# Transposes of q, k, softmax weights and the second half's x moved from TensorE to DMA in a hybrid attention and convolution layer on eight cores

## The reference, cut to what matters

```
h = RMSNorm(x) * pre_norm_g
p = h @ w_in + b_in          # q 1024 | k 128 | v 128 | attn gate 1024 | glu value 1024 | glu gate 1024 | conv gate 1024
attn = softmax over a causal window of 128 keys, with a sink logit per head,
       of rope(q) rope(k)^T / 8, times v; 16 query heads of 64, 2 key/value heads; times silu(attn gate)
hc   = value * sigmoid(gate); causal depthwise convolution of 31 taps + b_dw; LayerNorm over channels;
       silu; @ w_pw + b_pw; times silu(conv gate)
y = concat([attn, hc]) @ w_out + b_out
out = x + RMSNorm(y) * post_norm_g
```

## Time and profile before

| | us |
|---|---|
| median of 3 runs | 1105.13 (1103.37 to 1117.91) |
| profiled execution, its own time | 1108.99 |
| its span, core 2, first to last instruction | 1107.5 |
| span of the other cores | 1089.4 to 1099.1 |

### The profile page before, as it was taken

How to read it: one execution, slowest core, us unless ns; L and a number is a source line. 1 busy time by engine, 2 the same in 40 slices (tenths; PEclk the granted TensorE clock), 3 DMA queues, 4 the chain that set the end, 5 groups by cost and what they waited for, 6 DMA issues and landing times.

```text
span 1107.5 us, 17820 instructions; the slowest of 8 cores (1089.4 to 1107.5 us)
## 1 busy us (share of the span) xinstructions
PE 1034.8 (93%) x6848; PEld 543.7 (49%) x6906; DVE 531.1 (48%) x921; ACT 412.2 (37%) x1013; POOL 212.8 (19%) x215
## 2 busy tenths in 40 slices
PE   3799999899999999999999999989999999999996
PEld 1556444555555444445544644455655544444443
DVE  3566301466665355446636650045776636533434
ACT  2452112556555445034511212155565544402111
POOL 0260000134543320000000000012455341000000
PEclk9899999999999999999999999999999999999999
DMA  8874334655566589979499303344645657992445
GB/s 184 277 113 79 57 48 76 127 116 117 128 136 131 147 191 159 192 200 204 91 171 185 78 10 67 76 102 108 177 122 140 152 141 174 165 180 41 81 76 109
DMA packets 26533, 141.92 MB, mean 128 GB/s; under 512 B 5985, under 2 KB 6369, under 8 KB 15969
## 3 DMA queue, kind: packets, MB, share of 16 engines
q0 software_dynamic: 8784, 80.74, 43.1%
q1 hardware_dynamic: 17666, 60.04, 17.7%
HBM read 171.72 MB, written 32.51 MB: 184 GB/s over the span
## 4 chain that ended last, share of the span: by engine, by line
PE 73%; DMA 7%; SPq 6%; DVE 6%; ACT 3%; issue 3%; POOL 1%; ACTq 0%; DVEq 0%; POOLq 0%
PE psum L1144 19%; PE psum L775 10%; PE psum L1023 10%; SPq L152 6%; DMA arena<-arena 5%; PE psum L635 5%; PE psum L1113 5%; PE psum L869 4%; PE psum L818 4%; PE psum L828 4%; PE psum L631 3%; PE psum L593 2%; ACT arena L928 2%; PE psum L530 1%; PE psum L1182 1%
## 5 line engine op out<-in xcount | busy, mean ns | idle before, releaser
L1144 PE MATMUL psum<-arena 128*128 128x512 bf16 x939 | 207.2, 379 | 1.1
L1144 PEld LDWEIGHTS psum<-arena 128*128 128x128 bf16 x960 | 93.6, 98 | 111.3
L818 PE MATMUL psum<-arena 128*128 128x352 bf16 (+1 forms) x768 | 124.3, 316 | 0.0
L828 PE MATMUL psum<-arena 128*128 128x352 bf16 (+1 forms) x768 | 120.9, 311 | 3.4 <-ACT arena L831 3.3
L928 ACT ACTIVATE arena<-psum,arena 128x128 f32<-128x128 f32 x256 | 93.9, 367 | 61.4 <-DVE arena L918 43.6
L1023 PE MATMUL psum<-arena 128*128 128x512 bf16 x500 | 110.9, 379 | 4.3 <-ACT arena L1027 3.0
L775 PE MATMUL psum<-arena 128*128 128x512 bf16 x502 | 113.6, 387 | 0.5
L828 PEld LDWEIGHTS psum<-arena 128*128 128x128 bf16 x768 | 74.8, 98 | 42.9 <-issue 5.3
L818 PEld LDWEIGHTS psum<-arena 128*128 128x128 bf16 x768 | 72.5, 99 | 47.6 <-issue 12.7
L907 DVE COPY_PREDICATED psum<-arena,psum 128x1024 f32<-128x1024 uint16 x32 | 38.7, 1208 | 117.7 <-PE psum L901 117.7
L942 POOL TENSOR_TENSOR arena<-arena 128x1024 bf16<-128x1024 f32 x32 | 60.5, 1892 | 140.7 <-DVE arena L941 140.7
(11 more groups left out here) (129 smaller groups left out, 1282.9 us busy)
## 6 DMA issues: line engine op xcount, KB each, us to landing
arena<-w_in POOLq DMA_DIRECT2D x12, 2048.0 KB, 16.0
arena<-x_ext SPq DMA_DIRECT2D x18, 1024.0 KB, 10.6
arena<-w_in POOLq DMA_DIRECT2D x16, 1024.0 KB, 10.4
out<-arena POOLq DMA_DIRECT2D x15, 1024.0 KB, 9.2
arena<-w_out POOLq DMA_DIRECT2D x6, 2048.0 KB, 20.2
arena<-arena SPq DMA_DIRECT2D x64, 66.0 KB, 2.0
arena<-arena SPq DMA_DIRECT2D x64, 65.9 KB, 2.0
arena<-arena SPq DMA_DIRECT2D x64, 65.9 KB, 2.3
```

The lines of the kernel that those rows point to most:

```text
L818: cx.op('pe', lambda e, k=k: e.matmul(out=bank[bv][:, 0:n], lhsT=wbuf.ap[:, k, o:o + 128], rhs=xv[:, k, st:st + n], start=(k == 0), stop=( ...
L828: cx.op('pe', lambda e, k=k: e.matmul(out=bank[bg][:, 0:n], lhsT=wbuf.ap[:, k, o + 128:o + 256], rhs=xv[:, k, st:st + n], start=(k == 0), ...
L1144: cx.op('pe', lambda e, k=k: e.matmul(out=bank[b], lhsT=MIX.ap[:, k, j * 128:(j + 1) * 128], rhs=wo[n][k][0].ap[:, wo[n][k][1], :], start= ...
```

## The change

- `p1_b` for the second half: one DMA on SP from `xn` (128 x 2048) to XT1, `transpose=True`, in place of 16 transposes, an ACT copy and a DVE copy.
- `kv_b` and `q_b`, both halves: one transposing DMA on SP (128 x 256, 128 x 512) in place of 2 or 4 transposes and an ACT copy.
- Softmax weights: a new step `att_d` issues a transposing DMA of 128 x 1024 on SP from `pn` to a new tile `ptc` (two of them; the arena grows by 2 KB). `att_t` then has no PE part: its two DVE operations read `ptc` from SBUF, write `ptb` and, in place, `ptc`. For even units `att_d` comes right after `att_n`. For odd units it comes after the tick that follows the taps, and after 12 of the 16 shuffle DMAs; the other 4 follow it.
- PSUM bank 3 joins banks 0 and 1 in the rotation of GLU groups and taps.
- New DMA semaphores: 2 for q, 3 for k, 2 for the softmax weights, one for x.

The first half's x keeps its TensorE transposes. The whole diff:

```
--- before.py
+++ after.py
@@ -279,7 +279,7 @@
         O_KV = O_Z + 16384
         O_CV = O_KV + 7168
         O_AT = O_CV + 17920
-        ARENA = O_AT + 24576
+        ARENA = O_AT + 26624
         arena = cx.sb("arena", [128, ARENA], U8)
         BT = [T(f"blk{i}") for i in range(ARENA // BLK)]
 
@@ -370,6 +370,10 @@
         s_wo = [cx.dsem("wo0"), cx.dsem("wo1")]
         s_o = [cx.dsem("o%d" % i) for i in range(3)]
         s_x4 = cx.dsem("xr4")
+        s_qt = [cx.dsem("qt%d" % i) for i in range(2)]
+        s_kt = [cx.dsem("kt%d" % i) for i in range(3)]
+        s_pt = [cx.dsem("pt%d" % i) for i in range(2)]
+        s_xt = cx.dsem("xtr")
         s_rs = cx.dsem("rs")
         s_wh = [[cx.dsem("wh%d%d" % (i, h)) for h in range(2)] for i in range(2)]
         s_cp = cx.dsem("cp")
@@ -524,6 +528,11 @@
             return p1_n(s, j, n, bufs)
 
         def p1_b(s, j, xn):
+            if s == 1:
+                c0 = xcol(s, j)
+                cx.dma('sp', XT1.ap[:, :, c0:c0 + 128], xn.ap, s_xt, R=[xn],
+                       W=[xt_t[1][j]] + (xt_t[0] if j == 1 else []), transpose=True)
+                return
             bA, bB = nbank(), nbank()
             for k in range(16):
                 bb = bA if k < 8 else bB
@@ -600,17 +609,12 @@
                 cx.op('dve', lambda e: e.tensor_copy(
                     out=V.ap[:, j, :, :], in_=kf.ap[:, 128:256].rearrange("p (h d) -> p h d", d=64)),
                     R=[kf], W=[V_t[j]])
-                return kb
-
-            def kv_b(j, kb):
-                bt = nbank()
-                for g in range(2):
-                    cx.op('pe', lambda e, g=g: e.transpose(
-                        out=bank_bf[bt][:, g * 128:(g + 1) * 128], in_=kb.ap[:, g, :, :].rearrange("p a d -> p (a d)"),
-                        identity=ident_bf), R=[kb, cst_bf], W=[BK[bt]])
-                cx.op('act', lambda e: e.copy(
-                    out=kT.ap[:, :, j * 128:(j + 1) * 128],
-                    in_=bank_bf[bt][:, 0:256].rearrange("p (g n) -> p g n", n=128)), R=[BK[bt]], W=[kT_t[j]])
+                return kb, n
+
+            def kv_b(j, kbn):
+                kb, n = kbn
+                cx.dma('sp', kT.ap[:, :, j * 128:(j + 1) * 128], kb.ap.rearrange("p g a d -> p (g a d)"), s_kt[n % 3],
+                       R=[kb], W=[kT_t[j]], transpose=True)
 
             def q_h(b, j, wp, h):
                 c0 = xcol(s, j)
@@ -640,18 +644,12 @@
                     R=[BK[b], bq], W=[f])
                 rope(f.ap.rearrange("p (h d) -> p h d", d=64), b_.ap.rearrange("p (h d) -> p h d", d=64),
                      8, s * 8 + j, r1, r2, [f], [b_], E, 'pool' if E == 'pool' else 'dve')
-                return b_
-
-            def q_b(g, j, b_):
-                bt = nbank()
-                for t in range(4):
-                    cx.op('pe', lambda e, t=t: e.transpose(
-                        out=bank_bf[bt][:, t * 128:(t + 1) * 128], in_=b_.ap[:, t * 128:(t + 1) * 128],
-                        identity=ident_bf), R=[b_, cst_bf], W=[BK[bt]])
-                cx.op('act', lambda e: e.copy(
-                    out=MIX.ap[:, 4 * g:4 * g + 4, (j - 1) * 128:j * 128],
-                    in_=bank_bf[bt][:, 0:512].rearrange("p (t n) -> p t n", n=128)),
-                    R=[BK[bt]], W=[mix_t[4 * g + t][j - 1] for t in range(4)])
+                return b_, n
+
+            def q_b(g, j, bn):
+                b_, n = bn
+                cx.dma('sp', MIX.ap[:, 4 * g:4 * g + 4, (j - 1) * 128:j * 128], b_.ap, s_qt[n % 2],
+                       R=[b_], W=[mix_t[4 * g + t][j - 1] for t in range(4)], transpose=True)
 
             lag = []
 
@@ -785,7 +783,8 @@
 
             eb = [mk(O_AT + i * 4096, [8, 128], F32) for i in range(2)]
             pn = [mk(O_AT + 8192 + i * 2048, [8, 128], BF16) for i in range(2)]
-            ptb = [mk(O_AT + 12288 + i * 2048, [8, 128], BF16) for i in range(2)]
+            ptb = mk(O_AT + 12288, [8, 128], BF16)
+            ptc = [mk(O_AT + o_, [8, 128], BF16) for o_ in (14336, 24576)]
             ub = [mk(O_AT + 16384 + i * 2048, [512], F32) for i in range(2)]
             vb = [mk(O_AT + 20480 + i * 2048, [512], F32) for i in range(2)]
             ysum = [mk(O_MIX + 24576 + i * 2048, [512], F32) for i in range(2)]
@@ -793,7 +792,7 @@
             sq = [mk(O_MIX + 20480 + i * 2048, [512], F32) for i in range(2)]
             mixhi = [t for k in range(8, 16) for t in mix_t[k]]
 
-            rot["list"] = [0, 1]
+            rot["list"] = [0, 1, 3]
             if s == 0:
                 GRP = [(96, 0, 352), (448, 352, 352), (800, 704, 352)]
             else:
@@ -853,12 +852,12 @@
                     in1=cp[:, C_WDW + c * 32:C_WDW + (c + 1) * 32].rearrange("p (m g) -> p m g", g=4).unsqueeze(3)
                     .broadcast_to([128, 8, 4, 32]), op=ALU.mult), R=[cpb_], W=[dg])
 
-            def conv_shuffle(c):
+            def conv_shuffle(c, part):
                 hg = hglu[c % 2]
-                for g in range(4):
-                    for i in range(4):
-                        cx.dma('sp', rs.ap[32 * i:32 * (i + 1), g, 0:HW - i], hg.ap[32 * g:32 * (g + 1), i:HW],
-                               s_rs, R=[hg], W=[rs], group=True)
+                for q in (range(12) if part == 0 else range(12, 16)):
+                    g, i = q // 4, q % 4
+                    cx.dma('sp', rs.ap[32 * i:32 * (i + 1), g, 0:HW - i], hg.ap[32 * g:32 * (g + 1), i:HW],
+                           s_rs, R=[hg], W=[rs], group=True)
 
             def conv_taps(c, t2):
                 dg = diag[c % 2]
@@ -888,7 +887,7 @@
                     cx.op('pool', lambda e: e.tensor_tensor(out=qss.ap, in0=qss.ap, in1=sb_.ap, op=ALU.add),
                           R=[sb_, qss], W=[qss])
 
-            OB, TB = 2, 3
+            OB = 2
             SBK = [BK[i] for i in range(4, 8)]
             SV = psum[:, 2048:4096].rearrange("p (h k i) -> p h k i", h=8, k=2)
 
@@ -943,20 +942,20 @@
                     out=pu.ap, in0=eu.ap, in1=st["rden"].ap.unsqueeze(2).broadcast_to([128, 8, 128]), op=ALU.mult),
                     R=[eu, st["rden"]], W=[pu])
 
+            def att_d(ui):
+                pu, pc = pn[ui % 2], ptc[ui % 2]
+                cx.dma('sp', pc.ap, pu.ap.rearrange("p h k -> p (h k)"), s_pt[ui % 2], R=[pu], W=[pc], transpose=True)
+
             def att_t(ui):
-                pu = pn[ui % 2]
-                for h in range(8):
-                    cx.op('pe', lambda e, h=h: e.transpose(
-                        out=bank_bf[TB][:, h * 128:(h + 1) * 128], in_=pu.ap[:, h, :], identity=ident_bf),
-                        R=[pu, idn], W=[BK[TB]])
-                for i, m in ((0, mprev_bf), (1, mcur_bf)):
-                    cx.op('dve', lambda e, i=i, m=m: e.tensor_tensor(
-                        out=ptb[i].ap, in0=bank_bf[TB].rearrange("p (h q) -> p h q", q=128),
-                        in1=m.unsqueeze(1).broadcast_to([128, 8, 128]), op=ALU.mult),
-                        R=[BK[TB], cst_bf], W=[ptb[i]])
+                pc = ptc[ui % 2]
+                for o_, m in ((ptb, mprev_bf), (pc, mcur_bf)):
+                    cx.op('dve', lambda e, o_=o_, m=m: e.tensor_tensor(
+                        out=o_.ap, in0=pc.ap, in1=m.unsqueeze(1).broadcast_to([128, 8, 128]), op=ALU.mult),
+                        R=[pc, cst_bf], W=[o_])
 
             def att_o(ui):
                 g, j = units[ui]
+                pp = (ptb, ptc[ui % 2])
                 for kb in range(2):
                     kt = j - 1 + kb
                     for eh in range(2):
@@ -964,9 +963,9 @@
                             q4 = eh * 2 + dq
                             cx.op('pe', lambda e, kb=kb, kt=kt, eh=eh, dq=dq, q4=q4: e.matmul(
                                 out=bank[OB][32 * q4:32 * q4 + 32, :], lhsT=V.ap[:, kt, g, 32 * dq:32 * dq + 32],
-                                rhs=ptb[kb].ap[:, 4 * eh:4 * eh + 4, :].rearrange("p h q -> p (h q)"),
+                                rhs=pp[kb].ap[:, 4 * eh:4 * eh + 4, :].rearrange("p h q -> p (h q)"),
                                 start=(kb == 0), stop=(kb == 1), tile_position=(0, 32 * q4)),
-                                R=[V_t[kt], ptb[kb]], W=[BK[OB]])
+                                R=[V_t[kt], pp[kb]], W=[BK[OB]])
                 cx.op('dve', lambda e: e.tensor_tensor(
                     out=MIX.ap[:, 4 * g:4 * g + 4, (j - 1) * 128:j * 128],
                     in0=bank[OB].rearrange("p (t q) -> p t q", q=128), in1=arena_gate(g, j), op=ALU.mult),
@@ -986,6 +985,8 @@
                 for lag_, f in ((5, att_o), (4, att_t), (2, att_n), (0, att_s)):
                     if (n - lag_) >= 0 and (n - lag_) % 2 == 0 and (n - lag_) // 2 < 16:
                         f((n - lag_) // 2)
+                        if f == att_n and n % 4 == 2:
+                            att_d((n - lag_) // 2)
 
             wgc = [None, None]
             tick()
@@ -1008,12 +1009,14 @@
                 if c > 0:
                     conv_taps(c - 1, 0)
```

(6 more changed lines are left out.)

## The result

The changed kernel takes **1196.2 us** (median of 4 runs, 1194.4 to 1199.1), against 1104.25 of the kernel before beside it: ratio 1.083, 95% interval 1.078 to 1.088. The forecast was 1115 us in a range of 1078 to 1152: the change costs nine times what was forecast, and the time lies 44 us outside the range. Executions in which the cores of a die ran at a lower granted clock than the others are left out of all times here.

A forecast was written before the change was run, and what follows sets the result against it. The prediction took PE, busy 1034.8 of 1107.5 us, as the bound. Its terms, -9.0 - 7.4 - 2.3 - 4.5 + 13.8 + 19.5 = +10.1 us, on 1105.1 gave 1115 us, range 1078 to 1152.

The forecast's parts named there:

- x, -9.0 us: Second half's x in the output stage: eight sets of transposes leave PE and nothing there waits for XT, -9.0 us.
- The model of a DMA beside a load: GLU stage: a DMA issued behind the weight load takes 6.9 or 10.4 us, plus 0.9 for its bytes.
- q -7.4 and k -2.3: Projections: q saves 0.23 us in each of 32 tiles, -7.4; k saves half of 4.6 us, -2.3.
- rival 3: First half's k and q stages: late DMAs hold k and q buffers until PE waits, +10, 1125 us; chance 0.08.
- Second half's odd units, +13.8: Second half's GLU blocks: DMA behind the weight load lengthens the period from 21.8 to 24.1 us, six blocks, +13.8.
- First half's odd units, +19.5: First half's GLU blocks: DMA behind the load lengthens the period from 24.4 to 27.65 us, six blocks, +19.5.
- The eight units outside the loads, -4.5: GLU stages, eight units outside the twelve loaded blocks: each saves 0.56 us of transposes, -4.5 us.
- A transposing DMA alone takes 2.9 us: Softmax weights: 256 KB transposed moves like a plain copy, 2.0 + 0.9 = 2.9 us; upper bound 7.1.
- Rival 2: Odd units' masked copies: the transposing DMA is slow by itself, 4.2 us more at the upper bound, 1176 us; chance 0.22.
- rival 4: GLU units: the DMA's blocks go wholly one after another, 16 us a unit, 1260 us; chance 0.05.
- The third bank, 0: GLU groups and taps: the third PSUM bank removes only a few waits under 1 us, taken as 0 (0 to -3).

The follow-up runs named there:

- x alone: Only the second half's normed x by DMA, q, k and softmax weights transposed by TensorE as in the kernel before: 1159.0 us, ratio 1.049.
- q and k alone: Only q and k by DMA, x and softmax weights transposed by TensorE as in the kernel before: 1124.5 us, ratio 1.018.

## Why the prediction was wrong

- **x, -9.0 us, "nothing there waits for XT ... some 4 us after the issue, up to 10 behind an x load or a store": this step failed, and it is the largest error.** The first seven x tiles did take 4.3 to 10.8 us. But tile 8 goes out 2 us after three weight loads of together 4 MB, with three stores and the KV1 load to come, and took 79.0. PE needed it 47 us after its issue and stood 32 us. The prediction names x loads and stores beside x and no weight load, and not the bias load, which takes the place of `xn` and is held behind the DMA. x alone costs 53 us in this stretch where 9 were to be won; with q and k by DMA too it and the next cost 30.7 + 8.9.
- **It is not the only one.** With x back on TensorE the kernel still takes 1184.3 us, outside the range. The terms of x, q and k together are off by 57 us (-18.7 forecast, +38.4 measured by stages), those of the GLU stages by 22 (+28.8, +50.7).
- **The model of a DMA beside a load** (it waits for the load, then adds 0.9 us for its bytes) is right only for one load in long rows: there it landed mostly 1.1 to 1.2 us behind the load. With loads queued it is the number of rows that counts, each behind a row of the loads, and a transposing DMA holds SP meanwhile; the forecast worked with its bytes alone.
- **q -7.4 and k -2.3:** of these the second half's k and q group 1 were to give 1.2 + 1.8 = 3.0 us and gave 5.6; PE's wait for the last tile's rope, part of the 9.0 us that the earlier trace rows show before q's transposes, was left out. Elsewhere rival 3 came true, and more of it (q and k alone, core 3): k's first DMA behind the w_in load at 93.8 held DVE 13.3 us, of which PE felt 8.2, so its cover was some 5 us and not 17; and KV1, with q's DMAs beside it, reached PE 26.7 us late. q and k alone: +20 us, not -9.7.
- **Second half's odd units, +13.8: mechanism right, size off.** The period in loaded blocks is (983.64 - 826.74) / 6 = 26.15 us, forecast 24.1. The DMA went out at +8.3, not +7.7, since SP waits for POOL's scaling, and landed 9.3 us later, not 6.9 + 0.9: +17.6, and 17.6 + 9.0 - 0.35 = 26.25. The chain of 9.0 was right.
- **First half's odd units, +19.5:** period (393.13 - 228.96) / 6 = 27.4, forecast 27.65. The period was right, but the block of 24.4 us taken as the base was one of the longest: the six on that core average (372.02 - 231.15) / 6 = 23.5. So it is +3.9 a block, +23.4; the stage grew by 24.0 in the median of the cores.
- **The eight units outside the loads, -4.5: failed.** Without any load the stages are still 3.8 and 7.0 us longer than before, not 2.2 shorter; the masked copies, 0.88 us where I kept 0.69, are in the chain of every unit.
- **A transposing DMA alone takes 2.9 us: right,** 3.0 to 3.1. Rival 2 and rival 4 fall. The page "VectorE: DVE Perf Modes" of the Trainium skill (section "The three transpose paths") gives 1309 ns for one block; eight took 3.0 together, so such a figure cannot be multiplied.
- **The third bank, 0:** no run contradicts it, and none tried it alone.

Rival 2's time (1176) is the nearest of all, by luck: its condition, a DMA that is slow alone, did not come true.

## What to carry to other kernels

A DMA with many 256-byte rows shared the DMA engines row by row with whatever else was queued: count its rows against the length of the others' rows, and look for every load and store that is in flight until its landing, not only at its issue. Look at what stands behind its issue on the same queue, since a transposing DMA held that queue for most of its flight. Put such DMAs where a late landing has cover: away from queued loads, with free buffers and no reader near. Here what had to meet loads without such cover was better left on TensorE, even in a kernel that it bounds. And when TensorE's transposes are priced, count the wait before the last tile's and the clock behind it, not only their columns.

## What the runs showed of the hardware

- A transposing DMA of 256 KB from SBUF to SBUF lands in 3.0 to 3.1 us and holds SP 1.24 us; one of 512 KB beside queued weight loads took 79.0 and held SP 52.5. A plain copy in the same rows beside the same loads took 57.1 and held SP 0.6.
- The turn between the two queues: 556 packets of 9.2 KB against 555 of 256 bytes in 35 us; with load rows of 0.68 KB, 2,400 against 2,071 in 13 us, and the landing fell from 74.4 to 16.4 us.
- Loads suffer too: a KV1 load of 1 MB took 9.2 us before, 31.5 in the changed kernel, and 25.7 to 33.4 beside the transposed x tile where it took 9.7 to 16.1 beside the copied one.
- DVE's masked copies of 128x1024 bf16 from SBUF take 0.7 us each with POOL idle and 1.2 beside it, as against 0.69 from PSUM.
- A wait of 2.1 us of TensorE was followed by some 3.5 us at a granted clock of 0.50 on seven of eight cores (1.7 us lost).
